# Two weight products a slot in place of three in three of eight tiles, and the second half's attention, output and query stages one tile later

## The reference, cut to what matters

```python
def peer_ffn(h, w_query, sub_keys, u_tab, v_tab):       # 8 heads, top 16 of 16384 experts
    q = (hf @ w_query).reshape(M, H, 2, PEER_DQ // 2)
    s = jnp.einsum('mhpc,hpnc->mhpn', q, sub_keys)       # two lists of 128 scores a head
    top_s, top_i = lax.top_k(s, K)
    cand_s = top_s[:, :, 0, :, None] + top_s[:, :, 1, None, :]
    best_s, best_c = lax.top_k(cand_s.reshape(M, H, K * K), K)
    ids = jnp.take_along_axis(cand_i.reshape(M, H, K * K), best_c, axis=-1)
    g = jax.nn.softmax(best_s, axis=-1)
    ...
        u = jnp.take(u_tab, idb, axis=0)                 # 128 experts for every token
        v = jnp.take(v_tab, idb, axis=0)
        act = jax.nn.gelu(jnp.einsum('nkd,nd->nk', u, xb)) * gb
        return jnp.einsum('nk,nkd->nd', act, v)
```

## Time and profile before

| | |
|---|---|
| median of 3 runs | 3056.34 us (3051.41 to 3058.71) |
| the profiled execution's own time | 3051.98 us |
| its span, first to last instruction | 3050.2 us |
| busy: PE, PEld, DVE, ACT, POOL | 88%, 71%, 71%, 21%, 33% |
| moved by DMA | 1182.34 MB, mean 388 GB/s |
| of that the gathers | 1073.81 MB |

### The profile page before, as it was taken

One profiled execution on the slowest core, in us unless ns is written; L12 is line 12 of the kernel. 1 busy time (PEld: TensorE's weight loads), 2 busy tenths in 40 slices (PEclk: granted clock), 3 DMA queues, 4 the chain that ended last, 5 costly groups with the idle time before them and its releaser, 6 DMA issues.

```text
span 3050.2 us, 34985 instructions
## 1 busy us (share of the span) xinstructions
PE 2672.8 (88%) x11992; PEld 2179.5 (71%) x11992; DVE 2159.5 (71%) x6642; ACT 638.2 (21%) x1693; POOL 994.4 (33%) x1028
## 2 busy tenths in 40 slices
PE   8889999999977888989997898889997887777787
PEld 6778888788855776868876676768885556555555
DVE  1237777787877678777778668767779668779565
ACT  3221313712111205202111204301221101102001
POOL 0002323333233333333234333333234333433332
PEclk9899999999999999999999999999999999999999
DMA  5249999999999999999999999999999999999997
GB/s 183 98 148 405 381 383 397 390 406 407 390 403 427 405 425 393 402 426 407 390 409 423 427 427 405 392 427 407 405 380 423 427 426 422 424 416 417 427 424 332
DMA packets 166642, 1182.34 MB, mean 388 GB/s; under 512 B 19376, under 2 KB 19904, under 8 KB 23872
## 3 DMA queue, kind: packets, MB, share of 16 engines
q0 software_dynamic: 147456, 1073.81, 85.6%
q1 hardware_dynamic: 19008, 106.31, 9.0%
HBM read 1177.95 MB, written 2.10 MB: 387 GB/s over the span
## 4 chain that ended last, share of the span: by engine, by line
PE 59%; DMA 22%; DVE 11%; issue 7%; ACT 2%; POOL 0%; DVEq 0%; SPq 0%; ACTq 0%; POOLq 0%
PE main_bank L318 36%; DMA main_ring<-in_uv,main_idi 22%; PE main_bank L354 12%; PE main_bank L352 6%; DVE main_diagonal L301 3%; DVE main_ring L287 2%; PE main_bank L522 1%; DVE main_pick L193 1%; DVE main_hid L287 1%; PE main_bank L714 1%; DVE main_pick L199 1%; PE main_bank L730 1%; PE main_bank L722 0%; DVE main_topi L162 0%; DVE main_work L154 0%
## 5 line engine op out<-in xcount | busy, mean ns | idle before, releaser
L318 PE MATMUL main_bank<-main_ring,main_diagonal 128*128 128x256 f32 (+1 forms) x8160 | 1981.1, 389 | 337.5 <-DVE main_diagonal L301 335.0
L318 PEld LDWEIGHTS main_bank<-main_ring,main_diagonal 128*128 128x128 f32 x8160 | 1526.1, 192 | 713.5 <-DVE main_diagonal L301 495.7
L287 DVE CUSTOM_DVE_ANT_0 main_ring<-main_ring,main_bank 128x1024 f32<-128x1024 f32 x1024 | 1248.5, 1219 | 634.4 <-DMA main_ring<-in_uv,main_idi 624.2
L270 POOL DMA_INDIRECT main_ring<-in_uv,main_idi x1024 | 994.2, 971 | 2031.9 <-PE main_bank L318 1781.1
L292 ACT ACTIVATE main_act_out<-main_hid 128x1 f32<-128x1 f32 x1024 | 206.8, 203 | 2140.6 <-DVE main_hid L287 2133.1
L301 DVE TENSOR_SCALAR main_diagonal<-main_ident,main_act_out,main_gate 128x128 f32<-128x128 f32 x1024 | 359.6, 351 | 43.7 <-PE main_bank L318 23.8
L354 PE MATMUL main_bank<-main_xT,main_w_block 128*128 128x256 f32 x1408 | 350.2, 381 | 1.8 <-ACT main_xT L387 1.8
L354 PEld LDWEIGHTS main_bank<-main_xT,main_w_block 128*128 128x128 f32 x1408 | 267.6, 191 | 38.4 <-ACT main_xT L387 2.2
L354 PE MATMUL main_bank<-main_xT_query,main_w_block 128*128 128x256 f32 x512 | 122.9, 379 | 0.9 <-ACT main_xT_query L387 0.9
L354 PEld LDWEIGHTS main_bank<-main_xT_query,main_w_block 128*128 128x128 f32 x512 | 96.5, 190 | 13.9 <-ACT main_xT_query L387 1.2
L292 ACT ACT_TABLE_LOAD x81 | 103.9, 1283 | 1.4
(11 more groups left out here) (187 smaller groups left out, 1212.9 us busy)
## 6 DMA issues: line engine op xcount, KB each, us to landing
main_w_block<-in_w_query SPq DMA_DIRECT2D x32, 1024.0 KB
main_w_block<-in_w_ab SPq DMA_DIRECT2D x24, 1024.0 KB
main_ring<-in_uv,main_idi POOLq DMA_INDIRECT x1024
main_w_block<-in_w_c_in SPq DMA_DIRECT2D x16, 1024.0 KB
main_w_block<-in_w_out SPq DMA_DIRECT2D x8, 1024.0 KB
main_w_block<-in_w_c_out SPq DMA_DIRECT2D x8, 1024.0 KB
main_att_bias<-in_att_bias SPq DMA_DIRECT2D x16, 256.0 KB, 6.0
main_resid<-in_x SPq DMA_DIRECT2D x2, 1024.0 KB, 7.5
```

Of the source, the lines that this page charges most:

```text
L270: nc.gpsimd.indirect_dma_start(self.ring[n % self.bufs], None, self.uv[p // NT], bass.IndirectOffsetOnAxis(self.choice.idi[:, p % 2, k:k + ...
L287: self.nc.vector.tensor_tensor_reduce(out=row, in0=row, in1=self.ps[:, 6:8], scale=1.0, scalar=0.0, op0=ALU.mult, op1=ALU.add, accum_out=s ...
L318: last = self.nc.tensor.matmul(self.ps[:, 4 + at // T, at % T:at % T + wide], self.diagonal[:, n % DIAGS], self.ring[n % self.bufs][:, D + ...
```

## The change

`PACE` becomes a table by tile: 2 in tiles 0, 3 and 5, and 3 in tile 1. In tile 0 the query products start at slot 0 (2 before), the input projection's at `IN_AT` = 32 (24 before), so that the 256 products of the tile fill all 128 slots; the GLA steps stand 9 slots later or a little more. Attention leaves tile 0: it stands in tile 1 from slot 4 (`ATT_AT`), the output projection behind it at slot 50 and the queries at 78, both still at three a slot. In tiles 3 and 5 the output stays at slot 4 and the queries go from slot 32 to 44, at two a slot, so that they end in slot 107.

The choice's tables go by tile q now. Tile 1's choice starts in slot 97 of tile 0 and ends in slot 62 of tile 1; tile 2's starts in slot 91 of tile 1 and runs on to slot 24 of tile 2. For tiles 3, 5 and 7 the first two groups stand at slots 18 and 66 of the tile before (52 and 72 before); for 4 and 6 they stand at 65, 81, 97 and 113 (47, 60, 78 and 98 before).

```diff
-PAIR_AT = ((47, 60, 78, 98), (52, 72, 130, 150))
-HEAD_AT = ((45, 51, 58, 64, 76, 82, 96, 102), (52, 55, 72, 75, 130, 133, 150, 153))
-ATT_AT = 88
-PACE = 3
-def ends(first, b):
-    return first + (Weights.PIECES * (b + 1) - 1) // PACE
-def paced(k, first, count):
-    return range(max(0, PACE * (k - first)), max(0, min(count, PACE * (k - first + 1))))
+PAIR_AT = {1: (97, 118, 140, 172), 2: (93, 104, 120, 134), 3: (18, 66, 130, 150), 4: (65, 81, 97, 113)}
...
+IN_AT = 32
+ATT_AT = 4
+OUT_AT = {1: 50, 3: 4, 5: 4}
+ASK_AT = {1: 78, 3: 44, 5: 44}
+PACE = {0: 2, 1: 3, 3: 2, 5: 2}
+def ends(p, first, b):
+    return first + (Weights.PIECES * (b + 1) - 1) // PACE[p]
+def paced(p, k, first, count):
+    return range(max(0, PACE[p] * (k - first)), max(0, min(count, PACE[p] * (k - first + 1))))
...
@@ tensor @@
-                        if k == 2:
+                        if k == 0:
                             pe.wait_ge(norms.x_there, KD * 3)
-                        for x in paced(k, 2, 4 * weights.PIECES):
+                        for x in paced(p, k, 0, 4 * weights.PIECES):
                             tail0.pe_query_piece(pe, 0, 4 * weights.PIECES + x)
-                        for x in paced(k, 24, mix0.IN * weights.PIECES):
+                        for x in paced(p, k, IN_AT, mix0.IN * weights.PIECES):
                             mix0.in_piece(pe, 1, x)
...
+                    if p == 1:
                         u = (k - ATT_AT) // 2
                         if k % 2 == 0 and 0 <= u < 2 * AH + 2:
                             mix0.att_pe(pe, 1, u)
-                    if p == 1:
-                        if k == 0:
+                        if k == OUT_AT[p] - 4:
                             mix0.mix_turn_pe(pe, 1)
-                        if k == 4:
+                        if k == OUT_AT[p]:
                             mix0.out_wait_pe(pe, 1)
...
-                        for x in paced(k, 4, 4 * weights.PIECES):
+                        for x in paced(p, k, OUT_AT[p], 4 * weights.PIECES):
                             tail.pe_out_piece(pe, half, x, av if p > 1 else mix0.mixT[1])
-                        for x in paced(k, 32, PH * weights.PIECES):
+                        for x in paced(p, k, ASK_AT[p], PH * weights.PIECES):
                             tail.pe_query_piece(pe, half, x)
```

More of the change, by code:

```diff
@@ L1338, in _ @@
                     for q, at in sights(p, k):
-                        if at - 16 in PAIR_AT[q % 2]:
-                            choice.exponentials(act, q, PAIR_AT[q % 2].index(at - 16))
+                        if at - 16 in PAIR_AT[q]:
+                            choice.exponentials(act, q, PAIR_AT[q].index(at - 16))
                     if p == 0:
-                        if k in (19, 34, 47):
-                            choice.exponentials(act, 0, k // 14)
+                        if k in (20, 37, 52):
+                            choice.exponentials(act, 0, k // 16)
@@ L1344, in _ @@
                         for i in range(4, PH):
-                            if k == ends(2, i - 4) + 3:
+                            if k == ends(p, 0, i - 4) + 3:
                                 tail0.act_q(act, 0, i)
                         for i in range(3, PH):
-                            if k == ends(2, i - 4) + 7:
+                            if k == ends(p, 0, i - 4) + 7:
                                 tail0.act_scores(act, 0, i)
-                        for i in range(mix0.IN):
-                            if k == ends(24, i) + 3:
-                                mix0.in_act(act, 1, i)
@@ L1362, in _ @@
+                        if k == 86:
                             mix0.gla_silu_act(act, 1)
-                        if k in (69, 73):
-                            mix0.gla_out_act(act, 1, (k - 69) // 4)
-                        if k == 79:
+                        if k == 88:
                             mix0.gla_root_act(act, 1)
+                    for i in range(mix0.IN):
+                        if p * HK + k == ends(0, IN_AT, i) + 3:
+                            mix0.in_act(act, 1, i)
+                    if p == 1:
@@ L1371, in _ @@
                             mix0.att_keep_act(act, 1, u - 1)
-                    if p == 1 and k == 4:
-                        mix0.mix_turn_act(act, 1)
+                        if k == OUT_AT[p]:
+                            mix0.mix_turn_act(act, 1)
                     if p in tails:
@@ L1476, in _ @@
                         for g in range(choice.PAIRS):
-                            choice.step(dve, q, g, at - PAIR_AT[q % 2][g])
+                            choice.step(dve, q, g, at - PAIR_AT[q][g])
                     if p == 0:
-                        if k in (8, 15, 21, 26, 32):
-                            tail0.rank_dve(dve, 0, (8, 15, 21, 26, 32).index(k) + 3)
-                        if k in (10, 23, 35):
-                            choice.candidates(dve, k // 11 + (k == 10))
-                        if k in (12, 25, 38):
-                            choice.greatest(dve, k // 12)
@@ L1485, in _ @@
-                        if k in (14, 28, 41):
+                        if k in (9, 17, 25, 33, 41):
+                            tail0.rank_dve(dve, 0, k // 8 + 2)
+                        if k in (11, 27, 43):
+                            choice.candidates(dve, k // 16 + 1)
+                        if k in (13, 29, 45):
+                            choice.greatest(dve, k // 16 + 1)
+                        if k in (15, 31, 47):
                             choice.places(dve)
-                        if k in (16, 30, 43):
+                        if k in (17, 34, 49):
@@ L1488, in _ @@
                             choice.picked(dve)
-                        if k in (18, 33, 46):
-                            choice.numbers(dve, 0, k // 15)
-                        if k in (22, 37, 50):
-                            choice.gates(dve, 0, k // 16)
-                        if k == 40:
+                        if k in (19, 36, 51):
+                            choice.numbers(dve, 0, k // 17)
+                        if k in (23, 40, 54):
+                            choice.gates(dve, 0, k // 18)
@@ L1502, in _ @@
+                        if k == 74:
                             mix0.gla_states_dve(dve, 1)
-                        if k == 71:
+                        if k == 85:
+                            mix0.gla_squares_dve(dve, 1)
+                        if k == 90:
                             mix0.gla_gate_dve(dve, 1)
-                        if k == 78:
-                            mix0.gla_squares_dve(dve, 1)
-                        if k == 80:
+                        if k == 92:
                             mix0.gla_gated_dve(dve, 1)
-                        if k == 82:
+                        if k == 95:
```

68 lines of the change are left out of this document (38 added, 30 removed).

## The result

The changed kernel takes 3014.39 us (median of 4 runs, 3012.23 to 3021.48) against 3054.28 us before (4 runs, 3051.41 to 3058.71): a ratio of 0.9872, 95% interval 0.9851 to 0.9894, so about 40 us or 1.3% faster. A second set of five runs gave 3014.03 against 3058.11, 0.9845 (0.983 to 0.9859). The forecast was 3013 us.

What follows compares the result with a forecast made beforehand. PE was taken to bound slots with three products, the DMA narrowly those with two. Tile losses of 108.2 us fall to 67, 41 us gained, giving 3011 to 3015, stated as 3013 us; 8 in 10 within 2994 to 3037.

Steps and rivals of the forecast that it cites:

- The two floors of a slot: Per slot, two products need 2.69 us of PE with scores against 2.75 of DMA; three need 3.18 against 2.90.
- the sum: Lost DMA time over tiles 0 to 6: 67 us left of 108.2, so 41 us gained.
- Tile 0: Both floors level at 352 us; loss falls from 33.2 to 8 us, 5 for the GLA and 3 for the start.
- Tile 1: Loss rises from 17.4 to 29 us: attention brings 7.5, choice beside it 4; tile length 375 to 390 us.
- the 4 us for choice beside attention: Tile 1, slots 4 to 40: choice between attention's steps costs 4 us, between bounds of 0 and 19.
- Tiles 3 and 5: At two products a slot only the choice's loss remains: 5 us each, from 14.3 and 16.7.
- Tiles 2 and 4: Moving choice off the convolution and roots stretches leaves 11.5 and 7 us lost, from 14.6 and 10.5.
- the sign that PE's waits for diagonals would rise from 335 us: Sign of being right: PE's total waits for DVE's diagonals go up from 335 us.
- PE was to be no longer full in tile 0: Sign of being right: tile 0 at 355 to 365 us, 415 GB/s or more, PE no longer full.
- their signs: Tiles 3 and 5 at 345 to 352 us, with 420 GB/s or more in the query stage.
- the first rival: Choice bursts starve PE at two a slot; tiles 0, 3, 5 lose 11 us each; gain about 22, 3033 us; 24 in 100.
- The clock: Rule that thinner PE work halves the clock, making the kernel far slower: given 1 in 100.

Runs made afterwards that it cites:

- extra matmuls: Changed kernel with unread matmuls added, one more a slot in tile 6 and two in slots 48 to 127 of tile 7: 3024.57 us, ratio 0.9888.
- tiles 0 and 1 alone: Only tiles 0 and 1 changed, tiles 2 to 7 as in the kernel before except tile 2's choice as changed: 3040.87 us, ratio 0.9936.
- two such moves: Changed kernel with tile 1's third and fourth choice groups at its slots 40 and 56: 3011.90 us; or last group of tiles 4 and 6 at 126: 3014.48 us.
- three together: Changed kernel with tile 1's later groups behind attention, last group of tiles 4 and 6 at 126, second of 3, 5 and 7 at 60: 3007.95 us.

## Why the prediction was right

**What bounds the kernel.** The two floors of a slot, PE's sum and the DMA's, held. The extra matmuls are the direct proof, and setting the pace back in tile 0 costs 21.7 us and in tiles 3 and 5 24.8 us. Together that is more than the whole gain of 44 us on that chip, since the places of the choice were made for two a slot. By the count of losses tiles 0 and 1 give 16.9 of the 38.8 us, tiles 3 and 5 16.1 and tiles 2 and 4, where only the choice was moved, 8.0; tile 6 takes 2.2 back. Counting lost DMA time by tile forecast the sum to 3 us (69.4 against 67), and tiles 0 and 1 alone showed that the losses add. That most tiles came out within 2 us of the forecast is in part luck, since the same tile differs by more than that from execution to execution.

**Tile 0.** 8 forecast, 6.8 measured, with both floors level as forecast. PE's work was put at 352 us and is 352.54. The GLA's arrears are seen in slots 80 to 88 of the changed kernel:

```profile
448.10:473.90 25.80, 25.80 (x131) 21.92 (x130) 14.44 (x28) 6.39 (x14) 8.64 (x9) 1.00 0.92 369
```

25.8 x 58/427 = 3.5 us, half the tile's loss, in the slots in which PE needs 3.2 us each.

**Tile 1.** 29 forecast, 26.9 measured, and the 4 us for choice beside attention came out as 4. That the tile would take 375 to 390 us was wrong (370.8). 4.3 MB less move in it than before, 1.7 MB of gathers and 2.7 MB of other loads: attention's biases came in, but the keys and the norms' gains are loaded in other tiles now. The loss count allows for that, and the guess at the length did not.

**Tiles 3 and 5.** 5 each forecast, 5.8 and 9.1 measured. The cause is the one named (without the choice 1.6 each). The size was short in tile 5 (9.1, and 7.4 when the changed kernel was run again), whose slots 96 to 120 run at 388 GB/s with DVE at 54.6 of 64.9 us:

```profile
2274.10:2339.00 64.90, 58.14 (x275) 49.58 (x275) 54.61 (x216) 13.62 (x38) 23.19 (x24) 1.00 0.99 388
```

**Tiles 2 and 4.** 11.5 and 7 forecast, 10.0 and 7.1 measured. Alone in the kernel before, the move left 7.2 and 6.4.

**What was wrong.** First, the sign that PE's waits for diagonals would rise from 335 us: they fell to 300.3. PE's work is the same and the span shorter, so its idle time had to fall as a whole, by 30 us (3050.2 - 2672.8 before, 3010.4 - 2663.3 after). Most of it fell in tile 1, where PE was idle for 42.8 us and is for 15.6 now that attention stands there; in tile 0 it rose by 5 us.

Second, PE was to be no longer full in tile 0. Over the tile it isn't (352.5 of 363.1 us), but in slots 24 to 88 it is (181.65 of 182.1). Third, tiles 3 and 5 are slightly outside their signs (345 to 352 us and 420 GB/s): 353.8 and 352.4 us, and 417 GB/s in slots 48 to 112 of tile 3.

Fourth, the sum of the first rival is off by 3 us: 11 us in each of three tiles are 33, which is 15 and not 12 more than 8 + 5 + 5, so it stood for 3036 us. That rival, in which the choice takes PE's place, had its point in tiles 3 and 5, but for 14.9 us in the two together, not for the 22 it asked.

**The clock.** The mean granted clock is 0.99, 0.99 and 1.00 in tiles 0, 3 and 5, and 0.98 in tile 6 with PE busy for 253 of 316 us. The prediction read such means as if pauses never brought the clock down. They do, for a few us at a time, in both kernels: the earlier trace rows has 0.93 at the convolution, and tile 3 of the changed kernel has three such falls, of which this is the first. The lines are PE's timeline at two slots of tile 3, then the stretch of the fall:

```profile
1640.24 1.99 PE L318 MATMUL main_bank<-main_ring,main_diagonal 128*128 128x256 f32 x8 [0.43 <-DVE main_diagonal L301]
...
1532.64 3.68 PE L318 MATMUL main_bank<-main_ring,main_diagonal 128*128 128x256 f32 x8 [2.30 <-DVE main_diagonal L301]
...
1532.70:1536.10 3.40, 3.40 (x8) 2.75 (x9) 3.33 (x8) 0.69 (x2) 0.00 (x0) 0.50 1.01 429
```

PE had stood for 2.30 us, waiting for a diagonal behind a burst of the choice (a head and the picks of a group in one slot, 4.8 us of DVE); then the granted clock is 0.50, the 1.2 GHz level, and the slot's eight records take 3.68 us and not 1.99. The two other falls of the tile, at 1624.9 and 1645.4 us, stand behind pauses of 2.53 and 2.30 us. Not each such pause does it: PE stood 2.3 us at 2333.7 us, in tile 5, and no fall follows; tile 5 has none at all. By the rule of the Trainium skill (TensorE: Matmul & The Clock Gate, "Why this matters for your kernels") PE should not be idle for long between bursts of matmuls, or the clock drops back to half. The trace agrees in tile 3. Two products a slot don't bring the clock down by themselves: without the choice the mean of tiles 3 and 5 is 1.00. So a burst of the choice can cost PE twice, by the pause and by the lower clock behind it; how much of the tile's loss is the second, no run here separates.

## What to carry to other kernels

Where two engines share each step, write down both floors of a step and compare stages, not shares of the span: work that is the same in sum costs more where it is bunched over the other engine's floor. Spreading it, with the choice moved out of the way, was worth 40 us here with not one instruction less. Count the loss of the resource that is the last limit in each stage, since a stage can also get longer or shorter by bytes that move into or out of it. And once the first limit is met, moving one burst gains little or nothing that a measurement can tell (two such moves here), while three together gained some 6 us, so measure the sum of such moves too and not only each alone.

## What the runs showed of the hardware

PE can be filled from 80% to 95% of a tile that is bound by DMA at no cost that shows: 253 to 300 us busy of 316, and 0.1 us more. Above the DMA's time it costs the difference: 0.13 us in each of 80 slots, 10 us in all. The DMA's ceiling for gathers of 8 KB rows, alone or with weight blocks beside them, is 427 GB/s in every kernel here. The Trainium skill (HBM Reference, "Specifications (TRN2)") puts a core that streams alone at about 425 GB/s; the trace agrees. The granted clock can fall to its 1.2 GHz level behind a pause of PE of 2.3 us, in the middle of a stage whose mean reads 0.98 or 0.99, so a mean over a stage does not rule such falls out.
